# The triangular solver of an RWKV scan: sets cut by heads instead of steps, its first set moved to GpSimd, and loads of the scan moved to ScalarE's transfer queue

## The reference

```
def _rwkv_step(S, inp):
    r, w, kk, kka, kt, v = inp
    sk = jnp.einsum('bhij,bhj->bhi', S, kk)
    S = S * w[:, :, None, :] - sk[..., None] * kka[:, :, None, :] + v[..., None] * kt[:, :, None, :]
    return S, jnp.einsum('bhij,bhj->bhi', S, r)
```

## Time and profile before

| | us |
|---|---|
| median of 3 runs | 3848.86 (3847.08 to 3850.88) |
| the profiled execution's own time | 3855.86 |
| its span, first to last instruction | 3854.1 |
| TensorE busy | 3418.8 (89%) |
| VectorE busy | 1777.7 (46%) |
| ScalarE busy | 1198.2 (31%) |
| GpSimd busy | 506.0 (13%) |

### The profile page before, as it was taken

The page is one execution under the profiler, slowest core; times in us unless marked ns, Lnnn a source line. Parts: engine busy times, 40 slices in busy tenths (PEclk is TensorE's granted clock), DMA queues, the critical chain, the costliest instruction groups (busy, mean ns, idle before and its releaser), DMA issues.

```text
span 3854.1 us, 61577 instructions
## 1 busy us (share of the span) xinstructions
PE 3418.8 (89%) x26877; PEld 2310.1 (60%) x26877; DVE 1777.7 (46%) x2973; ACT 1198.2 (31%) x2097; POOL 506.0 (13%) x654
## 2 busy tenths in 40 slices
PE   6999989999999998756665999888989999989998
PEld 5777776343343866646654443237657788756787
DVE  4324641121223645965566122127755446845454
ACT  3225722111111656812231110004342234234233
POOL 2220120000000110036322000001102200102110
PEclk8999999999999998756887999999999999989999
DMA  6531147989887243978744999993213322202322
GB/s 243 185 108 52 60 176 266 375 324 367 328 320 268 105 163 123 305 194 209 175 138 171 342 418 419 420 384 106 77 45 116 100 74 87 101 33 88 118 68 77
DMA packets 332254, 744.34 MB, mean 193 GB/s; under 512 B 95128, under 2 KB 163488, under 8 KB 282832
## 3 DMA queue, kind: packets, MB, share of 16 engines
q1 hardware_dynamic: 293584, 696.14, 49.9%
q0 software_dynamic: 12096, 37.96, 3.2%
q10 hardware_dynamic: 26304, 6.30, 0.8%
HBM read 678.43 MB, written 61.89 MB: 192 GB/s over the span
## 4 chain that ended last, share of the span: by engine, by line
PE 72%; DVE 10%; DMA 9%; ACT 5%; issue 2%; ACTq 1%; POOL 0%; SPq 0%; DVEq 0%; POOLq 0%
PE ps L62 68%; DMA raw<-in_moe_w_dram 5%; PE ps L66 4%; DVE mx L75 2%; DMA mx<-Td 1%; DMA Td<-sT 1%; ACTq L120 1%; DVE o L75 1%; DVE o L81 1%; ACT cr L72 0%; ACT c L72 0%; DVE b L84 0%; DMA c<-in_w_in_dram 0%; DMA c<-in_w_ple_gate_dram 0%; DVE St L75 0%
## 5 line engine op out<-in xcount | busy, mean ns | idle before, releaser
L62 PE MATMUL ps<-raw,xinT 128*64 128x512 f32 (+1 forms) x4096 | 591.4, 492 | 24.1 <-DMA raw<-in_moe_w_dram 23.2
L62 PEld LDWEIGHTS ps<-raw,xinT 128*64 128x64 f32 (+1 forms) x4096 | 196.1, 123 | 392.0 <-issue 290.2
L62 PE MATMUL ps<-wp,hp 128*128 128x512 f32 x1024 | 316.4, 396 | 28.5 <-DVE mx L75 13.5
L62 PE MATMUL ps<-cr,oTr 128*128 128x512 f32 (+2 forms) x1024 | 255.5, 381 | 1.9 <-ACT oTr L72 1.5
L62 PEld LDWEIGHTS ps<-wp,hp 128*128 128x128 f32 x1024 | 193.1, 190 | 74.1 <-DVE mx L75 17.7
L75 DVE TENSOR_TENSOR mx<-mx,ps 128x512 f32<-128x512 f32 (+1 forms) x196 | 127.5, 663 | 222.8 <-PE ps L62 124.1
L62 PEld LDWEIGHTS ps<-cr,oTr 128*128 128x128 f32 x1024 | 187.6, 188 | 37.3 <-ACT oTr L72 2.0
L62 PE MATMUL ps<-wp,hTr 128*128 128x512 f32 x512 | 194.5, 389 | 0.0
L62 PE MATMUL ps<-raw,hidT 128*64 128x512 f32 x768 | 178.7, 604 | 3.2 <-DMA raw<-in_moe_w_dram 3.2
L62 PE MATMUL ps<-ar,naxh 128*128 128x512 f32 x576 | 147.8, 407 | 19.2 <-DVE ar L75 8.8
L75 DVE TENSOR_TENSOR wp<-c,wp 128x1536 fp32r<-128x1536 f32 x32 | 60.6, 1894 | 202.5 <-ACT wp L72 202.5
(11 more groups left out here) (532 smaller groups left out, 6374.1 us busy)
## 6 DMA issues: line engine op xcount, KB each, us to landing
raw<-in_moe_w_dram SPq DMA_DIRECT2D x384, 1024.0 KB, 8.2
c<-in_w_in_dram SPq DMA_DIRECT2D x28, 2048.0 KB, 9.1
mx<-in_ada_w_dram SPq DMA_DIRECT2D x14, 2048.0 KB, 8.0
raw<-in_ada_w_dram SPq DMA_DIRECT2D x8, 2048.0 KB, 13.4
a<-in_na_w_qkv_dram SPq DMA_DIRECT2D x6, 2048.0 KB, 8.1
c<-in_w_branch_dram SPq DMA_DIRECT2D x16, 512.0 KB, 5.9
c<-in_w_out_dram SPq DMA_DIRECT2D x4, 2048.0 KB, 11.0
c<-in_w_ple_gate_dram SPq DMA_DIRECT2D x4, 2048.0 KB, 7.8
```

The costliest lines, as they stand in the source:

```text
L62: return self.e.matmul(out, lhsT, rhs, start=start, stop=stop, skip_group_check=True) if self.e is not None else self
```

## The change

- A class `Solver` holds the solver; it is made before `rw_features`, so both stages use it.
- Sets are cut by heads and pairs of steps: set j has heads 0 to 7 (j even) or 8 to 15 (j odd) of steps 2(j//2) and 2(j//2)+1. Pass r needs set 2(r // 4) + r % 2. Squares and stores now take four transfers each, of 32 partitions, in place of two of 64.
- Set 0, which needs only feature units 0 to 7, is solved by GpSimd inside `rw_features`: SP loads its squares in C(8), and stores the result at the head of C(15), ahead of the last `Ad`, `Tb` and `Tk` stores.
- Set 1 is shared by columns: GpSimd columns 0 to 5 of all rows, VectorE the others (`SPLIT = 6`), rows 1 to 15 ahead of the grams of pass 0, rows 16 to 31 behind the first levels. GpSimd solves sets 2 to 5 alone. VectorE has no solver rows inside the passes.
- SP stores the solved sets (in passes 2, 4, 6, 7) and does `load_t`; ScalarE does neither.
- ScalarE's queue loads V and the token rows: 24 transfers at the head of the scan, then twelve in each pass from 1 to 10, between the Z copies and the x copy.
- SP's order at the head of the scan: `load_bk(0)`, the squares of set 1, `load_t(0)`, constants, the squares of sets 2 and 3, and then the `ar` rows of pass 0. V for the readout comes in four transfers (passes 3 to 6), the first output weights in pass 8.

The core of the diff:

```diff
-FIRST, LATE = 10, 24
+SPLIT = 6
+    def regions(self, j):
+        g, m = j % 2, j // 2
+        for z in range(2):
+            for i in range(2):
+                yield z, ORDER[z][2 * m + i], slice(8 * g, 8 * g + 8), slice(64 * z + 32 * i, 64 * z + 32 * i + 32)
+    def row(self, e, by, j, i, first, last):
+        P, m, w = self.P, 32 - i, last - first
...
+        e.tensor_tensor(pr, a, b, MUL).then_inc(*by.inc())
+        e.wait_ge(*by.last())
+        e.tensor_tensor(T[:, i:32, first:last], T[:, i:32, first:last], pr, SUB).then_inc(*by.inc('row', j, i))
# rw_features
     def pool(e):
+        e.wait_ge(*P.dve.at('features', 7))
+        inv.unit(e, 0)
+        for i in range(1, 32):
+            inv.row(e, P.pool, 0, i, 0, i)
         def C(n, kf, z):
+            if n == 15:
+                inv.store(e, 0)
...
+            if n == 8:
+                e.wait_ge(*P.dve.at('features', 7))
+                for i in (6, 7):
+                    e.wait_ge(*s_d[i % 2].at('dg', i))
+                inv.squares(e, 0)
# rw_scan_order
-    rows(0, 1, 31)
-    store(0)
-    load_t(0)
+    blocks(0)
+    rows(1, 1, 15)
     for s in range(4):
         gram(0, s)
+    level(0, 0)
     recur(0, 0, 'x1')
...
     level(0, 1)
+    rows(1, 16, 31)
+    store(1)
+    for j in range(2, 6):
+        rows(j, 1, 31)
     for r in range(12):
-        if more and not whole:
+        if more and r != 4:
             load_t(r + 1)
         if more and r:
             load_m(r + 1)
         if r + 2 < 12:
             load(r + 2)
+        rows_in(r)
+        if r in (2, 4, 6, 7):
+            store({2: 2, 4: 3, 6: 4, 7: 5}[r])
+        if r == 4:
+            load_t(r + 1)
# rw_scan, ScalarE
+            for i in (13, 14, 15):
+                e.wait_ge(*s_t[i % 3].at('T', i))
+            load_tm(e, 0)
             fence(P, e, 'rw_features', *stored)
+            load_v(e, 0)
+            load_v(e, 1)
+            load_tm(e, 1)
+        def load_m(r):
+            if r >= 2:
+                e.wait_ge(*P.pe.at('recur', r - 2))
+                load_v(e, r)
+                load_tm(e, r)
# rw_scan, VectorE
+        def solve(j, i):
+            if j == 1 and i > SPLIT:
...
+                inv.row(e, P.dve, j, i, SPLIT, i)
# rw_scan, GpSimd
+            inv.row(e, P.pool, j, i, 0, min(SPLIT, i) if j == 1 else i)
# rw_scan, SP
+            load_bk(0)
             for s in s_d:
                 e.wait_ge(*s.at('all'))
+            e.wait_ge(*P.dve.at('features', 15))
+            inv.squares(e, 1)
+            load_t(0)
             fence(P, e, 'rw_features', *stored)
...
+            for j in (2, 3):
+                inv.squares(e, j)
+        def store(j):
+            inv.store(e, j)
+            if j in (2, 3):
+                refill(j)
```

More of the change, by code:

```diff
@@ L2756, in rows @@
         e.dma_start(self.V[:, 5, :], bc(I['rw_ln_b'][0])).then_inc(*self.s_lg.inc('readout'))
-        e.wait_ge(*P.dve.at('row', 5, 31))
-        e.wait_ge(*P.sig("td5_out").at('td', 5))
+        e.wait_ge(*P.pool.at('row', 5, 31))
+        for j in (4, 5):
+            e.wait_ge(*P.sig(f"td{j}_out").at('td', j))
         for c in (1, 2, 3, 0):
@@ L2761, in rows, with rw_scan_order @@
         self.s_g.name('readout')
-def rw_scan_order(const, load, load_m, load_t, gram, blocks, level, recur, solve, store, refill, read, rows_in):
+def rw_scan_order(const, load, load_m, load_t, gram, blocks, level, recur, solve, store, read, rows_in):
     reads = iter(READ)
@@ L2772, in one, with rows @@
                 read(*x)
-    def rows(n, first, last):
+    def rows(j, first, last):
         for i in range(first, last + 1):
-            solve(n, i)
+            solve(j, i)
     const()
@@ L2781, in rw_scan_order @@
         load_m(r)
-    rows(0, 1, 31)
-    store(0)
-    load_t(0)
+    blocks(0)
+    rows(1, 1, 15)
     for s in range(4):
         gram(0, s)
+    level(0, 0)
     recur(0, 0, 'x1')
[L2788 to L2791, removed]
     level(0, 1)
+    rows(1, 16, 31)
+    store(1)
+    for j in range(2, 6):
+        rows(j, 1, 31)
     for r in range(12):
-        more, n = r + 1 < 12, (r + 1) // 2
-        whole = more and r % 2
-        if more and not whole:
+        more = r + 1 < 12
+        if more and r != 4:
             load_t(r + 1)
@@ L2811, in rw_scan_order @@
             gram(r + 1, 1)
[L2812 to L2815, removed]
             gram(r + 1, 2)
@@ L2869, in rw_scan @@
     s_tm = [P.sig(f"tm{i}_in") for i in range(2)]
-    s_sa = [P.sig(f"sa{i}_in") for i in range(6)]
-    s_td = [P.sig(f"td{n}_out") for n in range(6)]
+    s_td = inv.s_td
     s_vu = [P.sig(f"vu{i}_in") for i in range(2)]
@@ L2913, in skip, with tokens, load_tm, load_v @@
         pass
[L2915 to L2935, removed]
-        for z in range(2):
-            e.dma_start(A_of(n)[64 * z:64 * z + 64], Ad[z][:, ORDER[z][n], :].rearrange("(q i) s -> q i s", i=32)).then_inc(*s_sa[n].inc())
-        s_sa[n].name('sa', n)
+    def tokens(r, z, c):
+        return slice(chunk(r, z) * 128 + 64 * c, chunk(r, z) * 128 + 64 * c + 64), slice(group(r) * 512, group(r) * 512 + 512)
+    def load_tm(e, r):
+        for z in range(2):
+            for c in range(2):
+                t, f = tokens(r, z, c)
+                e.dma_start(tm(r, z)[half(c), c, :], Tm['b', z][t, f]).then_inc(*s_tm[r % 2].inc())
+                e.dma_start(tm(r, z)[half(1 - c), c, :], Tm['k', z][t, f]).then_inc(*s_tm[r % 2].inc())
+        s_tm[r % 2].name('tm', r)
+    def load_v(e, r):
+        for z in range(2):
+            for c in range(2):
+                t, f = tokens(r, z, c)
+                e.dma_start(VU(r, z)[half(c), cut(z, c), :], vd[t, f]).then_inc(*s_vu[r % 2].inc())
+        s_vu[r % 2].name('vu', r)
     def pe(e):
@@ L3133, in recur @@
                 e.wait_ge(*P.pe.at('y', r, 1))
-                e.wait_ge(*s_td[0].at('td', 0))
+                for j in range(2):
+                    e.wait_ge(*s_td[j].at('td', j))
                 for yo, src in parts(r):
@@ L3137, in recur @@
                 P.act.name('y', r)
[L3139 to L3156 removed]
+        def load_m(r):
[3 more added lines that the diff above has]
+                load_tm(e, r)
+        rw_scan_order(const, skip, load_m, skip, skip, skip, level, recur, skip, skip, lambda *r: R.act(e, *r), skip)
         P.end('rw_scan', P.act)
@@ L3304, in rows_in @@
                 R.rows(e)
-        rw_scan_order(const, load, load_m, skip, skip, skip, skip, skip, skip, skip, refill, lambda *r: R.sp(e, *r), rows_in)
+        rw_scan_order(const, load, skip, load_t, skip, skip, skip, skip, skip, store, lambda *r: R.sp(e, *r), rows_in)
     P.stage(pe, act, dve, pool, sp)
```

171 lines of the change are left out of this document (90 added, 81 removed).

## The result

The changed kernel takes **3895.32 us** (3891.83 to 3901.17, 4 runs) against 3849.87 (3847.08 to 3852.58, 4 runs) before: ratio **1.0121**, 95% interval 1.0107 to 1.0136. It is slower, as forecast, but by 45 us where I had forecast 12, and outside my range (3834 to 3882).

A forecast was written before the change was run, and what follows sets the result against it. In the scan neither TensorE nor VectorE was full, so waits set the pace. Features and start +13 us plus passes 1 to 10 at 0, taken as 12, gave 3868 profiled and a median of 3861 us, range 3834 to 3882.

The forecast's parts named there:

- Turns in the features, +11: Last five feature units: VectorE and GpSimd exclude each other on SBUF, 0.3 us per VectorE instruction, +11 us.
- SP stands at the store of set 0 until 1665: End of the features: SP reaches this store at about 1661 and waits for GpSimd, which ends at 1665.
- First level 1706, x2 of pass 1 at 1735 (+13): Start of the scan: late ar rows and set 1 delay pass 1's x2 from 1721.9, +13 us including the features' 11.
- The waits for sets, −46.7 + 3 for set 3: Passes 1 to 10: TensorE's five waits for turned blocks go, 46.7 us; set 3 comes 3 us late in pass 4.
- Twelve issues, +59 gross (5.9 in each of ten passes): Head of passes 1 to 10: twelve loads on ScalarE's queue hold the copy of x, costing 5.9 us a pass.
- Rival 2: Copy of x at each pass's head: ScalarE's issues run beside existing waits, passes 4.4 us shorter, total 3825; chance 0.15.
- give back 1.5 of each pass from TensorE's issue waits, which the idle time should hide: Passes 1 to 10: idle time hides TensorE's own issue waits, taking 1.5 us off each pass.
- My bounds for the passes, 12 either way: Passes 1 to 10 together: forecast 269 against 268.5 us, so 0 change, with bounds −12 and +12.
- The base: Whole kernel: profiled execution 3855.9 us for a span of 3854.1, 7 above the median 3848.9; 3868 profiled gives median 3861.
- the 13 that I rounded to 12: Whole kernel: sum of +13 for features and start and 0 for the passes, of which 12 us was taken.

The follow-up runs named there:

- e3: Kernel before, with GpSimd doing 62 unused solver-size products and differences in the features from unit 10 on: 3861.95 us, ratio 1.0023.
- e6_head: Changed kernel with set 0 stored behind the last Ad, Tb and Tk stores and the squares of sets 2 and 3 last in SP's start order: 3890.01 us.
- e2_before_act: Kernel before, with only the twelve V and token-row loads of each pass moved from SP's to ScalarE's queue: 3909.92 us, ratio 1.0153.
- e9: Kernel of e8 with the feature transfers of passes 7 to 11 cut to a quarter of their bytes: 3828.78 us, ratio 0.9935.
- e10: Changed kernel with the feature transfers of passes 7 to 11 cut to a quarter of their bytes: 3879.10 us, ratio 1.0073.
- e14: Kernel before with GpSimd solving sets 1 (from row 11) to 5, SP storing them, plus an unawaited 1 MB transfer in passes 0 to 9: 3836.79 us.
- e5: Changed kernel with ScalarE's twelve load issues spread in three groups of four behind its copies of x and u: 3860.94 us, ratio 1.0026.
- e8: Changed kernel with ScalarE's issues spread in groups of four, SP's new start order, and set 3 stored in pass 3: 3848.18 us, ratio 0.9994.
- e7: Changed kernel with only V's four issues per pass left on ScalarE and the eight token rows back on SP: 3849.05 us, ratio 0.9995.

## Why the prediction was wrong

By its own steps:

- **Turns in the features, +11:** right. +11.7 in the trace (last VectorE product 1657.6 against 1645.9), +9.6 in the time by e3 alone; 0.3 us an instruction, as I took.
- **SP stands at the store of set 0 until 1665:** right (1666.48).
- **First level 1706, x2 of pass 1 at 1735 (+13):** 1712.75 and 1740.51 (+18.6). Short by 5.6. Set 1's squares took 8.7 us to land where I had 6.2, and SP's four square loads, four block loads and eight square loads took 6.6, 5.4 and 8.3 us where I counted 20 us for everything to the ar rows, which began at 1699.06. e6_head shows that with the store of set 0 and the squares of sets 2 and 3 put last the x2 of pass 1 comes 9.1 us earlier. (The prediction's 13.4 us "from the landing of set 0's store to the level" run from the store's start at 1684.82; it landed at 1689.82. The sum used them as from the store, so nothing changes by it.)
- **The waits for sets, −46.7 + 3 for set 3:** −39.8. Right but for set 3, whose wait was 6.9 us, 3.9 more than I took.
- **Twelve issues, +59 gross (5.9 in each of ten passes):** right. The la waits rose by 53.8, and by 71.6 in e2_before_act, where the time rose by 57.6. Rival 2 (cover, not cost) is out: it wanted the copy held under 5 us, and it was held for 9.0.
- **"give back 1.5 of each pass from TensorE's issue waits, which the idle time should hide":** this is the step that failed. It took 15 us off; they rose by 13.7. These 29 us are more than the whole miss in the passes (20.4 against 0); the waits for VectorE's results gave some back (those for `St` and `GG` fell from 17.0 to 1.9). I read "issue" as a delay inside the engine that any idle time absorbs. It is the wait for the next block of instructions, whose packet begins late behind data (e9, e10, e14 and the count over all traces), and it grows where TensorE stands little elsewhere (e5, e8). My bounds for the passes, 12 either way, had no case in which these waits grow. TensorE's busy time also rose by 8.6 us for the same 5368 matmuls, which I had at nothing; the mean granted clock is 0.78 in both, and why it rose is open.
- **The base:** the span rose by 36.9 us (3854.1 to 3891.0), the median by 45.5: the profiled execution before was 7 above its median, and the one after was not. I took it as the same for both; that is 8.6 us.

Together: start 5.6, passes 20.4, 1 for the 13 that I rounded to 12, less 2.1 at the end of the scan (x2 of pass 11 at +39.0, span +36.9), and 8.6 of the base; with 1.0 for the median of before in this comparison, 34 between 3861 and 3895. That the kernel came out slower was no luck: the start of the scan, where I had all of the loss, gave 18.6 of the 36.9 us of the span.

## What to carry to other kernels

A transfer issue holds its engine's own work for some 0.7 us, so it is free only in a gap that is there: four ahead of a copy that TensorE waits for nearly fitted (6.5 us of waits in ten passes), twelve cost 40 us. A wait removed is not the gain: when the long ones went, TensorE ran into the supply of its own instructions, which the page books as "issue"; look at the instruction queue's row before giving anything back there. And take from a large change the one part that the trace asks for: GpSimd solving whole sets ahead of their passes, with the stores and `load_t` out of the way of the copy of x, was worth 27 us, while the change as a whole came out 73 above that.

## What was new about the hardware

- GpSimd's memsets beside VectorE's two-input products cost these nothing (951 ns against 950); GpSimd's products and differences cost them 0.33 us each.
- TensorE's instructions come as 16 KB packets, 43 in ten passes, among the data on the same DMA engines; of 254 issue waits 245 ended 2.2 to 3.2 us after such a packet began. The longest was 6.7 us, in e7.
- The packet behind an issue wait began 1.1 us after its end (median) with the DMA engines under 30% busy, 2.4 us after it and up to 10.2 with them over 95% busy.
- The place of these stands is fixed by the program, not by time: 245 of the 254 lie a multiple of 256 TensorE records apart, and four kernels stood at the same matmul of pass 3.
